# Router logits as two half-height matrix products in two PSUM banks

## What is computed

```python
h = h + mixed @ w_out
u = rms(h, norm2_g)
g_logits = u @ w_group + b_group        # 4 columns
f_logits = u @ w_fine + b_fine          # 32 columns
# group = argmax(g_logits); the two best fine logits of that group select the experts
```

## Time and profile before

| | us |
|---|---|
| median of 3 runs (lowest, highest) | 4329.56 (4327.42, 4331.07) |
| the profiled execution | 4338.74 |
| its span, first to last instruction | 4337.0 |
| TensorE busy in the span | 4111.1 (95%) |
| VectorE busy | 2823.5 (65%) |
| ScalarE busy | 2488.2 (57%) |

### The profile page before, as it was taken

How to read it: one execution, slowest core, us unless ns; L and a number is a source line. 1 busy time by engine, 2 the same in 40 slices (tenths; PEclk the granted TensorE clock), 3 DMA queues, 4 the chain that set the end, 5 groups by cost and what they waited for, 6 DMA issues and landing times. The chain is left out here.

```text
span 4337.0 us, 83225 instructions
## 1 busy us (share of the span) xinstructions
PE 4111.1 (95%) x27983; PEld 3112.2 (72%) x27985; DVE 2823.5 (65%) x3211; ACT 2488.2 (57%) x3370; POOL 688.2 (16%) x916
## 2 busy tenths in 40 slices
PE   8999989997999999999998999869999999999997
PEld 6888867774555555555555888758888888888886
DVE  3222235668998998999996555476666655555665
ACT  4222225557887887887886333246666655545665
POOL 0000002221000000000001111003332333223332
PEclk9999999998999999999999999979999999999999
DMA  5444443313111112111102344247666654555674
GB/s 202 182 144 177 152 173 122 111 68 115 31 32 59 31 31 60 31 31 53 36 7 99 141 155 155 97 169 255 222 243 225 223 204 166 204 195 198 242 262 143
DMA packets 308629, 590.32 MB, mean 136 GB/s; under 512 B 38704, under 2 KB 104240, under 8 KB 308400
## 3 DMA queue, kind: packets, MB, share of 16 engines
q1 hardware_dynamic: 257568, 460.82, 30.2%
q0 software_dynamic: 46224, 118.03, 7.9%
q10 hardware_dynamic: 4608, 8.39, 0.5%
HBM read 427.75 MB, written 209.72 MB: 147 GB/s over the span
## 5 line engine op out<-in xcount | busy, mean ns | idle before, releaser
L1171 DVE TENSOR_TENSOR_SCAN att_R<-att_stay,att_R,att_turn 128x1025 f32<-128x1025 f32 x448 | 1024.7, 2338 | 19.1 <-ACT att_stay L1105 19.0
L1115 ACT ACTIVATE att_RT<-att_rt 128x1024 f32<-128x1024 f32 (+1 forms) x576 | 550.4, 956 | 241.4 <-PE att_rt L1053 205.6
L1053 PEld LDWEIGHTS att_rt<-ident,att_R 64*128 64x128 f32 x8448 | 320.2, 139 | 369.5 <-issue 369.3
L1105 ACT ACTIVATE att_stay<-att_z 128x1024 f32<-128x1024 f32 (+2 forms) x576 | 546.6, 949 | 6.0 <-PE att_z L1039 5.6
L1068 PE MATMUL att_out<-att_RT,att_dv 128*64 128x512 f32 (+3 forms) x2304 | 523.7, 576 | 0.0
L1053 PE MATMUL att_rt<-ident,att_R 64*128 64x64 f32 x8448 | 388.0, 228 | 79.2 <-ACT att_RT L1115 65.0
L1619 DVE TENSOR_TENSOR ew_lo<-ew_raw,ew_hi 128x1024 fp32r<-128x1024 f32 x384 | 443.9, 1218 | 22.1 <-ACT ew_hi L1612 13.3
L1612 ACT ACTIVATE ew_hi<-ew_raw 128x1024 fp32r<-128x1024 f32 x384 | 374.0, 1048 | 100.2 <-PE ex_down L2007 93.5
L236 PE MATMUL qkv_out<-u_u_hi,qkv_w_hi 128*128 128x512 f32 x768 | 308.8, 402 | 3.6 <-DVE u_u_lo L227 3.6
L236 PE MATMUL qkv_out<-u_u_hi,qkv_w_lo 128*128 128x512 f32 x768 | 300.6, 391 | 0.0
L236 PE MATMUL qkv_out<-u_u_lo,qkv_w_hi 128*128 128x512 f32 x768 | 300.0, 391 | 0.0
(11 more groups left out here) (282 smaller groups left out, 8303.6 us busy)
## 6 DMA issues: line engine op xcount, KB each, us to landing
ew_raw<-in_w_e_gate SPq DMA_DIRECT2D x32, 2048.0 KB, 9.0
ew_raw<-in_w_e_up SPq DMA_DIRECT2D x32, 2048.0 KB, 9.7
ew_raw<-in_w_e_down SPq DMA_DIRECT2D x32, 2048.0 KB, 9.1
u_x<-in_x SPq DMA_DIRECT2D x32, 512.0 KB, 5.9
s_u_hi<-u_u_hi SPq DMA_DIRECT2D x8, 2048.0 KB, 11.8
s_u_lo<-u_u_lo SPq DMA_DIRECT2D x8, 2048.0 KB, 16.4
mix_x<-in_x SPq DMA_DIRECT2D x32, 512.0 KB, 4.9
s_h<-mix_h SPq DMA_DIRECT2D x32, 512.0 KB, 3.7
```

The lines of the kernel that those rows point to most:

```text
L1053: last = nc.tensor.transpose(rt[:, half, qt, h, :], R[lanes, n % 3, qt, h, s * P:(s + 1) * P], k.ident[lanes, lanes])
L1105: done = nc.scalar.activation(stay[:, step % 4, :, 0:width], z_pair[:, :, 0:width], ACT.Sigmoid, scale=-scale)
L1115: nc.scalar.activation(RT[:, s, first:, :, :, :].rearrange("p t h half q -> p (t h) half q"), turned_pair, ACT.Copy).then_inc(rt_copied, 1)
L1171: nc.vector.tensor_tensor_scan(joined(R[:, n % 3, s, :, :]), joined(stay[:, step % 4, :, :]), joined(turn[:, s, :, :]), R[:, (n - 1) % 3, ...
```

## The change

Each product over 128 channels becomes two over 64, one on the lower and one on the upper half of the array's rows. The lower half's sums go to the bank `logits`, the upper half's to the first 36 columns of the bank `tr[0]`, which is free at that point. VectorE adds the bias to the first, waits for that, and then adds the second bank to the row.

```diff
+            logits_biased = sem("mix_logits_biased")
...
             def pe_logits(pe, T, t):
                 pe.wait_ge(u2_t_ready, T + 2)
                 pe.wait_ge(logits_ready, T + 1)
                 for c in range(DC):
-                    last = nc.tensor.matmul(logits[:], u2_t[:, t % 2, c, :], w_router[:, c, :],
-                                            start=(c == 0), stop=(c == DC - 1))
+                    for half in range(2):
+                        lanes = slice(half * HD, (half + 1) * HD)
+                        last = nc.tensor.matmul((logits[:], tr[0][:, 0:NR])[half], u2_t[lanes, t % 2, c, :],
+                                                w_router[lanes, c, :], start=(c == 0), stop=(c == DC - 1))
                 last.then_inc(logits_done, 1)
...
             def dve_logits(dve, T, t):
                 dve.wait_ge(logits_done, T + 3)
-                nc.vector.tensor_tensor(k.logits[:, t * NR:(t + 1) * NR], logits[:], k.b_router[:], ALU.add).then_inc(logits_ready, 1)
+                row = k.logits[:, t * NR:(t + 1) * NR]
+                nc.vector.tensor_tensor(row, logits[:], k.b_router[:], ALU.add).then_inc(logits_biased, 1)
+                dve.wait_ge(logits_biased, T + 1)
+                nc.vector.tensor_tensor(row, tr[0][:, 0:NR], row, ALU.add).then_inc(logits_ready, 1)
```

## The result

| | us |
|---|---|
| changed kernel, median of 6 runs (lowest, highest) | 4344.52 (4339.79, 4348.5) |
| kernel before, median of its 6 runs | 4331.51 |
| ratio, 95% interval | 1.0024, 1.0014 to 1.0034 |
| ratio in a second, longer series (11 runs of it) | 1.0021, 1.0012 to 1.0030 |
| span of the profiled execution | 4340.2 |

The change makes the kernel slower by 0.24% in the one series and by 0.21% in the other, 10.4 and 9.1 us (0.0024 and 0.0021 of some 4332). The forecast was 4341.5 us, 11.9 more than before.

What follows compares the result with a forecast made beforehand. TensorE, at the rate of its weight loads in the logits, was taken as the bound. 30 x 0.38 + 0.45 = 11.9 us on the median of 4329.56 gave 4341.5 us, range 4337 to 4351.

Steps and rivals of the forecast that it cites:

- What bounds the stage: In `mix`, TensorE is always busy, so whatever its queue grows by, the kernel grows by; logits run at weight-load rate.
- The pair of loads: At the logits, loads on the two array halves run side by side, 0.113 us per pair.
- The two passes of a float32 product: At the logits, their order across the halves might cost one more step, 0.11 us per tile.
- Rival (a): At the logits, the halves do not load side by side: 2.13 us more per tile, 4394 us; chance 0.05.
- Rival (b): At the logits, alternate halves load at the transposes' rate, 0.062 us per pair: faster, 4317 us; chance 0.07.
- The changes of shape: Around the logits, entering and leaving 64*128 drains TensorE: 0.32 us in, 0.24 out, +0.34 per tile with the pairs.
- Rival (c): Around the logits, 128*128 and 64*128 follow without a drain: 0 to 0.1 us, kernel 4330 to 4333 us; chance 0.10.
- The term of 0.38 us per tile: At the logits of 30 tiles, 0.34 us plus allowances makes 0.38 each, 11.4 us in all; range 0.34 to 0.61.
- the allowances for lag and for the pair: At the logits, 0.01 to 0.04 us for the second half's lag, and 0.001 per pair above 0.112.
- VectorE: Behind the logits, its second addition, 0.25 us per tile, is hidden and costs nothing; 8 us if cover were gone.
- The end of the stage: Behind the last tiles of `mix`, additions and lag come into line, together 0.45 us.
- the second last tile's 0.1: At the 31st logits, TensorE waits for VectorE's `u2`, and about 0.1 us comes through.

Runs made afterwards that it cites:

- e3: The changed kernel with its two loops exchanged, all eight lower-half products first, then all eight upper: 4442.33 us, ratio 1.0250.
- e4: The kernel before with each logits product cut by tokens into two of 64 array columns (128*64), one bank, one addition: 4317.19 us, ratio 0.9965.
- e2: The kernel before with only the lower half (64 rows) of each logits product made, one bank, one addition: 4413.43 us, ratio 1.0186.
- e6: The changed kernel with its products in two visits, chunks 0 to 3 moved inside the second projection half: 4352.82 us, ratio 1.0035.
- e1: The changed kernel with full-height products, even ones in one bank, odd in the other, both additions kept: 4335.01 us, ratio 1.0007.

## Why the prediction was right, and where it was off

*What bounds the stage.* Right. TensorE is busy for all of the stretch in both kernels, and what its queue gains the kernel gains: the stage grew by 8.4 us, the medians by 10.9 (4345.4 - 4334.54) and 13.0 (4344.52 - 4331.51), the ratios by 9.1 and 10.4.

*The pair of loads.* Right: 0.111 against the 0.113 taken, and 0.01 of lag. The two passes of a float32 product on one half, then on the other, cost no extra step. Rival (a), the halves one after another, fell with it; e3 shows what it looks like, and that it needs the products to stand in blocks. Rival (b), the halves at 0.062, fell too: with fewer rows no load of these products became shorter, and e4 shows that half the columns do it. What spoke for it was in part misread. Of the eight loads in the earlier trace rows the first was taken ahead under the projection; the other seven are these:

```profile
2611.36 0.79 PEld L1402 LDWEIGHTS mix_tr<-ident,mix_u 128*128 128x128 f32 x7
```

That is a step of 0.108 ((0.79 - 0.14)/6) and not 0.126. And the loads of the transposes are recorded as 0.14 us long at full height and at half height alike, those of the logits as 0.19 at both. The shorter load thus goes with the transpose and not with the height. Whether the pair's 0.062 comes from the height or from the 64 columns moved in place of 128 was not tested.

*The changes of shape.* Right in mechanism and size: 0.32 on the way in and 0.24 on the way out, as forecast, in every tile. Rival (c), no drain between 128*128 and 64*128, is refuted by the 0.35 us without a load before each first pair, and before the first load in e2 and the first pairs in e6 too; e4 has the same between 128*128 and 128*64. E2 and e6 show that these changes are the cost: half of the work with the same two changes costs the same, and four changes cost twice.

*The term of 0.38 us per tile.* This is what was mis-sized. A tile grew by 0.286 us in 29 of 31 distances, 25% less. Of the difference, 0.05 are the allowances for lag and for the pair, of which next to nothing came (the logits took 2.23 in place of 2.24). The other 0.04 are given back behind the logits: the sums and the first dozen projection matmuls run closer together than before. From the sums' first load to the first full projection step it is 0.78 us (2606.99 to 2607.77), where it was 0.80; the rest goes in steps of 0.01 to 0.02 in the next 2 us. Which queue catches up there was not tested.

*VectorE.* Right. The forecast put the end of the two additions 0.06 us ahead of the reciprocal; it is 0.04 (2621.89 and 2621.93), and e1 carries the additions without loss. *The end of the stage*: 0.23 us for the second addition, as forecast at 0.25. From the last tile's sums to the last `select` instruction it is 0.2 us more in all; forecast 0.45, since the second last tile's 0.1 and the lag did not show.

In place of the sum, 30 x 0.38 + 0.45 = 11.9, the stage shows 29 x 0.286 = 8.3 and 0.1 from its two ends together. The medians' 13.0 and 10.9 lie nearer to the forecast than the stage does; what the medians hold beyond the stage's 8.4 us, be it noise or the clock of the last section, was not in the forecast, so that nearness is in part luck. The forecast of slower by more than 0.2% held in the estimates, 0.24% and 0.21%, but both intervals reach below 0.2%: the trace's 8.4 us is right at that bound.

## What to carry to other kernels

A short stage in a shape of the array of its own paid some 0.3 us here for going in and out, with all of the work (2 x 64 rows) as with half of it; put neighbours into the same shape, or stay out unless the stage gains more than that. Where weight loads are the limit, cut them by columns (the stationary operand's free side), not by rows: half the rows changed nothing, while half the columns halved the step (0.058 for 0.111) and brought the logits from 1.90 us to 1.37 with both changes of shape paid, and the results stay in one bank. And after such a gain look at once for who is late next; here VectorE's `select`, hidden before, came through with 0.3 us.

## What the runs showed that was not expected

TensorE's granted clock fell behind logits at half height, though the profile counts TensorE as busy without a pause. In e3, where one half of the array works at a time for 3.3 us, the clock is at 0.50 (1.2 GHz) behind the logits (2521 to 2523) and the stretch from 2364 to 2800 has a mean of 0.89; in e2, where the upper half rests for 2.2 us, it fell in 11 of 31 tiles, 1.6 us each, with a mean of 0.96; in the changed kernel, with both halves at work, behind no tile's logits in one profiled execution and twice in the other (0.68 over 5.3 us from 2406.7, and 0.50 from 2797.3 to 2800.7); at full height, with column halves and in e6, whose visits are half as long, in no tile from 2390 to 2750. What in the half-height work lets the clock fall was not tested by itself. This adds a cost to the change that its first profile, taken in an execution without such a tile, does not show, and that may be part of the difference between 8.4 us in the stage and 9 to 13 in the medians. How often it happens outside the profiled executions was not measured.
